# Expert output bias: from a small product in every expert block to one product of gates and bias rows behind the last block

## What is computed

```python
def moe(h, w_router, b_router, w1, b1, w2, b2):
    logits = (xf @ w_router) + b_router
    top_val, top_idx = lax.top_k(logits, TOP_K)        # 4 of 32
    gates = jax.nn.softmax(top_val, axis=-1)
    ...
    def expert_block(args):
        tok, e = args
        xb = xf[tok]
        act = clamped_swiglu(xb @ w1[e] + b1[e])
        return act @ w2[e] + b2[e]
    y = lax.map(expert_block, ...)
    y = y * buf_g[:, None]                             # each row times its gate
    out = jax.ops.segment_sum(y, buf_tok, num_segments=T)

h = h + moe(rmsnorm(h, ffn_norm), ...)
h = rmsnorm(h, final_norm)
```

## Time and profile before

| what | value |
|---|---|
| median of three runs | 1431.04 us |
| profiled execution, its own time | 1431.11 us |
| its span, first to last instruction | 1429.3 us |
| PE busy | 1302.9 us, 91% |
| DVE, ACT, POOL busy | 670.1, 291.4, 284.3 us |
| DMA, mean | 322 GB/s |
| granted clock of TensorE, mean | 0.963 |

### The profile page before, as it was taken

One profiled execution on the slowest core, in us unless ns is written; L12 is line 12 of the kernel. 1 busy time (PEld: TensorE's weight loads), 2 busy tenths in 40 slices (PEclk: granted clock), 3 DMA queues, 4 the chain that ended last, 5 costly groups with the idle time before them and its releaser, 6 DMA issues.

```text
span 1429.3 us, 36690 instructions
## 1 busy us (share of the span) xinstructions
PE 1302.9 (91%) x13312; PEld 623.7 (44%) x13313; DVE 670.1 (47%) x2257; ACT 291.4 (20%) x578; POOL 284.3 (20%) x455
## 2 busy tenths in 40 slices
PE   4999999989288997899999999997999899999992
PEld 2655666555233442344444444442444344444441
DVE  3015333664644553355555555553455355555555
ACT  3102223432011111111111111111111111111113
POOL 5400000000012222122222222222222122222221
PEclk9999999999589999999999999998999999999996
DMA  9520001617478999999999998999999999999995
GB/s 317 157 50 1 1 1 63 236 27 312 158 313 337 415 417 418 419 416 416 417 418 417 417 417 319 378 413 417 419 416 417 422 416 417 417 418 417 415 416 185
DMA packets 59808, 459.65 MB, mean 322 GB/s; under 512 B 8420, under 2 KB 8804, under 8 KB 27012
## 3 DMA queue, kind: packets, MB, share of 16 engines
q1 hardware_dynamic: 51220, 436.63, 73.8%
q0 software_dynamic: 8176, 22.36, 6.0%
q10 hardware_dynamic: 384, 0.26, 0.1%
HBM read 440.72 MB, written 18.51 MB: 321 GB/s over the span
## 4 chain that ended last, share of the span: by engine, by line
PE 83%; DMA 9%; DVE 4%; issue 2%; ACT 1%; POOL 0%; SPq 0%; DVEq 0%; POOLq 0%; ACTq 0%
PE PS L1546 37%; PE PS L1573 19%; DMA sb_arena<-in_w 7%; PE PS L1227 4%; PE PS L1233 4%; PE PS L1583 2%; PE PS L1230 2%; PE PS L1231 2%; PE PS L1422 2%; PE PS L1447 1%; PE PS L1521 1%; PE PS L1589 1%; PE PS L1553 1%; PE PS L1329 1%; PE PS L1395 1%
## 5 line engine op out<-in xcount | busy, mean ns | idle before, releaser
L1546 PE MATMUL PS<-sb_arena,sb_work 128*32 128x512 f32 x5184 | 586.7, 603 | 35.3 <-DMA sb_arena<-in_w 28.6
L1546 PEld LDWEIGHTS PS<-sb_arena,sb_work 128*32 128x32 f32 x5184 | 174.2, 111 | 398.1 <-issue 347.4
L1573 PE MATMUL PS<-sb_arena,sb_work 128*32 128x256 f32 x5184 | 296.5, 380 | 4.6
L1129 DVE TENSOR_SCALAR sb_work<-PS 128x256 f32<-128x256 f32 x81 | 34.4, 425 | 395.8 <-PE PS L1553 395.8
L1573 PEld LDWEIGHTS PS<-sb_arena,sb_work 128*32 128x32 f32 x5184 | 166.3, 110 | 111.1 <-issue 19.4
L769 ACT ACTIVATE sb_work<-PS 128x256 f32<-128x256 f32 x81 | 31.1, 384 | 810.9 <-PE PS L1583 810.9
L1142 DVE TENSOR_SCALAR sb_work<-PS,sb_gates 32x256 f32<-32x256 f32 x324 | 155.2, 479 | 15.0 <-PE PS L1573 0.8
L534 POOL TENSOR_TENSOR sb_sm<-sb_sm 128x1 f32<-128x1 f32 x85 | 16.9, 199 | 676.9 <-DVE sb_gidx L1120 676.9
L1097 DVE TENSOR_SCALAR sb_slots<-sb_ca,sb_b,sb_rk 128x128 bf16<-128x128 f32 x344 | 96.5, 370 | 59.0 <-issue 58.2
L543 POOL DMA_INDIRECT accd<-sb_work,sb_sidc x81 | 111.1, 1371 | 12.5 <-issue 1.1
L767 ACT ACT_TABLE_LOAD x81 | 103.9, 1283 | 1.4
(11 more groups left out here) (246 smaller groups left out, 1165.8 us busy)
## 6 DMA issues: line engine op xcount, KB each, us to landing
sb_arena<-in_w SPq DMA_DIRECT2D x192, 2048.0 KB
sb_arena<-in_w_in SPq DMA_DIRECT2D x6, 2048.0 KB, 21.4
sb_arena<-in_x SPq DMA_DIRECT2D x8, 512.0 KB, 9.6
sb_arena<-in_w_out SPq DMA_DIRECT2D x2, 2048.0 KB, 13.1
accd<-sb_arena SPq DMA_DIRECT2D x4, 512.0 KB, 7.6
xfd<-sb_arena SPq DMA_DIRECT2D x4, 512.0 KB, 5.8
sb_arena<-accd SPq DMA_DIRECT2D x4, 512.0 KB, 5.0
out<-sb_arena SPq DMA_DIRECT2D x4, 512.0 KB, 3.5
```

The costliest lines, as they stand in the source:

```text
L1546: last = mm(PS[group(c), b, :].rearrange("p (a n) -> p a n", a=2), xT[:, k % 2, group(k // 2)], w[:, k, :, c, :], start=k == 0, stop=False)
L1573: last = mm(PS[group(n), 4, 0:QD], actT[:, k % 2, group(k // 2)], w[:, k, n * QD:(n + 1) * QD], start=False, stop=k == KT - 1)
```

## The change

The bias `b2` no longer enters the blocks. `ball` keeps the two parts of `b1`; POOL splits two thirds of the rows that it split before. The gates of a tile are now kept in `gk` ([128 tokens, 32 experts] for each of four tiles). Between the routing and the first block PE turns them (four transposes into PSUM bank 0) and ACT copies the result to `gT` ([32, 512]). In a block the four products at L1589 are gone, and the first product of `down` starts the sum.

Behind the last block SP loads `b2` as it is ([32, 1024], 128 KB) ahead of the final gain. PE multiplies: for each token tile and each half of the columns `gT` times `b2` (eight products, 32 rows deep, 512 columns wide, one PSUM bank each), then for each of the same eight banks the identity times the loaded rows of `accd` (128 rows deep), which adds those rows to the bias in PSUM. ACT squares from PSUM and no longer from SBUF, and DVE's product with the gain reads PSUM and waits until ACT has read the tile (`fin_sq`), since both read the same banks.

```diff
@@ SP
+            sp.wait_ge(gT_done, 1)
             w1_load(1, 1)
...
             sp.wait_ge(up_done, nb)
+            sp.dma_start(fb2, I["b2"]).then_inc(b2_in, 16)
             sp.dma_start(fgain, I["final_norm"].to_broadcast([P, D])).then_inc(acc_in, 16)
@@ POOL
-            for c in range(3):
-                src = I["b1"][:, c * D:(c + 1) * D] if c < 2 else I["b2"]
-                pool.dma_start(bchunk, src).then_inc(bch_in, 16)
+            for c in range(2):
+                pool.dma_start(bchunk, I["b1"][:, c * D:(c + 1) * D]).then_inc(bch_in, 16)
@@ ACT
+            act.wait_ge(gT_done, 1)
+            act.activation(gT[:, :], PS[0:NE, 0, :], ACT.Copy).then_inc(gT_ready, 1)
             xT_copy(0, 0)
...
             act.preload_act_table_set("natural_log_exp_and_others")
+            act.activation(sm[:, 20:21], ones1, ACT.Copy).then_inc(copies_over, 1)
             for u in (0, 2):
                 for t in (u, u + 1):
-                    act.wait_ge(x_in[t], 48)
-                    act.activation(fsq[:, t, :], fh[:, t, :], ACT.Square, accum_out=ss[:, t:t + 1]).then_inc(fin_sq, 1)
+                    act.wait_ge(sum_done, t + 1)
+                    act.activation(fsq[:, t, :].rearrange("p (b n) -> p b n", b=2), PS[:, 2 * t:2 * t + 2, :],
+                                   ACT.Square, accum_out=ss[:, t:t + 1]).then_inc(fin_sq, 1)
@@ DVE
-                step(nc.vector.tensor_reduce(gd, ohg.rearrange("p k e -> p e k"), AX.X, ALU.add))
+                nc.vector.tensor_reduce(gk[:, t, :], ohg.rearrange("p k e -> p e k"), AX.X, ALU.add)\
+                    .then_inc(gk_ready, 1)
+                dve.wait_ge(gk_ready, t + 1)
...
+            nc.vector.memset(nx, 0.0).then_inc(rows_over, 1)
             dve.wait_ge(acc_in, 16)
-            for u in (0, 2):
-                for t in (u, u + 1):
-                    dve.wait_ge(x_in[t], 48)
-                    nc.vector.tensor_tensor(fg[:, t, :], fh[:, t, :], fgain, ALU.mult).then_inc(fin_gain, 1)
+            for t in range(TT):
+                dve.wait_ge(fin_sq, t + 1)
+                nc.vector.tensor_tensor(fg[:, t, :].rearrange("p (b n) -> p b n", b=2), PS[:, 2 * t:2 * t + 2, :],
+                                        fgain.rearrange("p (b n) -> p b n", b=2), ALU.mult).then_inc(fin_gain, 1)
@@ PE, down and finish_block
-                                  w[:, k, n * QD:(n + 1) * QD], start=False, stop=k == KT - 1)
+                                  w[:, k, n * QD:(n + 1) * QD], start=k == 0, stop=k == KT - 1)
...
                 pe.wait_ge(sel_ready, g + 2)
-                for n in range(Q):
-                    mm(PS[group(n), 4, 0:QD], selb[:, b, :], ball[:, 2 * D + n * QD:2 * D + (n + 1) * QD],
-                       start=True, stop=False)
                 pe.wait_ge(actT_ready, g + 1)
@@ PE, ahead of the blocks
+            pe.wait_ge(gk_ready, TT)
+            for t in range(TT):
+                last = nc.tensor.transpose(PS[0:NE, 0, t * P:(t + 1) * P], gk[:, t, :], ident)
+            last.then_inc(gT_done, 1)
             turn_x(0, 0, 0)
             slot_product(1)
+            pe.wait_ge(gT_ready, 1)
@@ PE, behind the blocks
+            pe.wait_ge(b2_in, 16)
+            for t in range(TT):
+                if t == 2:
+                    pe.wait_ge(rows_over, 1)
+                    pe.wait_ge(copies_over, 1)
+                for n in range(2):
+                    mm(PS[:, 2 * t + n, :], gT[:, t * P:(t + 1) * P], fb2[:, n * 512:(n + 1) * 512],
+                       start=True, stop=False, skip_group_check=True)
+            for t in range(TT):
+                pe.wait_ge(x_in[t], 48)
+                for n in range(2):
+                    last = mm(PS[:, 2 * t + n, :], ident, fh[:, t, n * 512:(n + 1) * 512],
+                              start=False, stop=True, skip_group_check=True)
+                last.then_inc(sum_done, 1)
```

More of the change, by code:

```diff
@@ L189, in build @@
         fg = arena[:, 9 * D:13 * D].rearrange("p (t d) -> p t d", t=TT)
+        fb2 = arena[0:NE, 13 * D:14 * D]
         wo = slot(2)
@@ L229, in build @@
         rt = left[:, 656:664]
+        gk = arena[:, o - HF * NKEY:o - HF * NKEY + P].rearrange("p (t e) -> p t e", t=TT)
         work = sb("work", [P, 5 * 512])
@@ L279, in build @@
         ident = ca[:, C_ID:C_ID + P]
-        ball = sb("ball", [P, 3 * D], BF16)
+        ball = sb("ball", [P, 2 * D], BF16)
+        gT = sb("gT", [NE, T])
         g6 = sb("g6", [P, TT, NE, 6], BF16)
@@ L341, in build @@
         added = sem("added")
+        gk_ready, gT_done, gT_ready = sem("gk_ready"), sem("gT_done"), sem("gT_ready")
+        b2_in, rows_over, copies_over, sum_done = sem("b2_in"), sem("rows_over"), sem("copies_over"), sem("sum_done")
         w1_full = [[sem(f"w1_full{par}{c}") for c in range(4)] for par in range(2)]
@@ L1020, in _ @@
                 step(nc.vector.tensor_tensor(ohg, e4.unsqueeze(2).to_broadcast([P, TOPK, NE]), oh, ALU.mult))
-                step(nc.vector.tensor_reduce(gd, ohg.rearrange("p k e -> p e k"), AX.X, ALU.add))
-                step(nc.vector.tensor_copy(g6[:, t, :, 0], gd))
-                step(nc.vector.tensor_tensor(gd, gd, g6[:, t, :, 0], ALU.subtract))
+                nc.vector.tensor_reduce(gk[:, t, :], ohg.rearrange("p k e -> p e k"), AX.X, ALU.add)\
+                    .then_inc(gk_ready, 1)
+                dve.wait_ge(gk_ready, t + 1)
+                step(nc.vector.tensor_copy(g6[:, t, :, 0], gk[:, t, :]))
+                step(nc.vector.tensor_tensor(gd, gk[:, t, :], g6[:, t, :, 0], ALU.subtract))
                 step(nc.vector.tensor_copy(g6[:, t, :, 1], gd))
```

## The result

The changed kernel takes 1456.11 us (median of 4 runs, 1455.39 to 1460.86) beside 1431.39 us for the kernel before on the same chip (4 runs, 1430.64 to 1434.6): a ratio of 1.0177, with a 95% interval of 1.0158 to 1.0197. The forecast was 1441.8 us, its range 1437.0 to 1447.5. The direction was right; 14 us were missing.

What follows compares the result with a forecast made beforehand. PE was taken to set the time in 52 blocks, the DMA engines from 930 to 1132 and up to 579 us. Terms 0 + 0 + 10.8 on a median of 1431.04 gave 1441.8 us, range 1437.0 to 1447.5.

Steps and rivals of the forecast that it cites:

- A loss is excluded, since nothing is added to a block: Expert blocks, four products removed: no loss possible, at most 0.09 or 0.18 us gained a block.
- Edit 1: Four products less in each of 81 blocks: 0 us.
- they fill a wait that stays when they go: Before `down` in a block: the four products only fill the wait for ACT's copy, so removing them gives 0.
- Its own sign: In a block of the profile after: `down` still starts 0.17 to 0.18 us behind the end of ACT's copy.
- 52 blocks that PE sets: Two stretches, 582 to about 920 us (29 blocks) and 1135 to 1401 us (23), where PE alone sets the time.
- The DMA engines set it from 930 to 1132: Expert blocks from 930 to 1132 us: the DMA engines, not PE, set the time.
- Edit 2: Work ahead of the blocks (four transposes, ACT's copy, waits): hidden in PE's 5.0 us idle gap, 0 us.
- Edit 3: The end, PE's 32 float32 passes, then square and gain product: the end moves by +10.8 us.
- the 2.1 us for the clock's rise: PE's passes at the end: 2.1 us added to 14.0 because the clock starts at half after idle time.
- The rival for it: At the end, products only 32 rows deep leave the clock at half: 6.9 us more, 1448.7; chance 0.09.
- new code on PE: PE's new instructions behind the loop aren't at hand: up to 5.5 us more, 1447.3; chance 0.10.
- the stall at 437 us: PE's 5.48 us issue stall falls otherwise with another code length: up to 5.5 us back, 1436.3 to 1441; chance 0.07.

Runs made afterwards that it cites:

- the wait for w2 first: The changed kernel with the wait for w2 and its register work ahead of the wait for ACT's copy: 1449.08 us, ratio 1.0127.
- every wait on a row of its own: The kernel before with the wait for w2's first half and its register work moved to the second of the four products: 1425.34 us, ratio 0.9954.

## Why the prediction was wrong

- **"A loss is excluded, since nothing is added to a block"** is the step that failed in Edit 1, and it put 0 to 0.18 us of gain where there was 0.11 of loss. The count of products was right, and so was "they fill a wait that stays when they go"; but I listed instructions and not the waits that they carry. One of the products carried a wait, the order of instructions with its waits showed where it would go, and I had read that order without them. The runs show it both ways: the wait without the loss of products (+8.6 us by the ratio), the products back without the loss (6.8 us less than the changed kernel by medians that were not taken side by side, 7.3 by the ratios). Its own sign (`down` 0.17 to 0.18 us behind the end of ACT's copy) came out as 0.29.
- **Where a block counts.** I took 52 blocks that PE sets, which would make 5.7 us at 0.109 each. The loss came in every one: from the block at 581.98 (580.95 with the change) to the last at 1400.31 (1406.71) there are 68 blocks, 818.33 and 825.76 us, 7.4 more, 0.109 each. "The DMA engines set it from 930 to 1132" was thus wrong for a loss: the waits for weights stayed as long as they were (28.6 and 27.2 us in all), only later. That each load waits for a buffer that PE's block frees would explain it; no run took that apart. A gain came through in part: between the same two blocks the trace with 11.74 us a block takes 0.5 us more than that of the kernel before instead of 2.7 less (581.69 to 1400.48), and those with 11.65 take 4.8 (with products, 584.93 to 1398.46) and 7.1 less (without, 581.79 to 1393.04) where 68 blocks would give 8.8.
- **Edit 2, 0**: 1.0 us off. The first `up` took 8.42 us instead of 9.05, the granted clock from 394 to 400 was 0.58 instead of 0.50, and the first block's copy came at 414.71 instead of 415.77. The new transposes stand shortly before; whether they did it wasn't tried, and the time at 581 varies by more between runs (584.93 in one).
- **Edit 3, +10.8**: the count of passes, the chain of square and gain product, the arrival of the rows and the start 7.3 us behind the last `down` all held. The step that failed is the 2.1 us for the clock's rise, which measured 8.9 (22.9 us for the 32 passes instead of 16.1): I took it from products 128 rows deep, and "the depth of 32 rows instead of 128 changes nothing in the count of columns" is true and beside the point. The rival for it was there, with the right price (6.9 forecast, 6.8 measured) and a chance of 0.09, on the argument "no row has them". No row is no evidence for either side, and a chance nearer one half would have been honest.
- **The sum.** Forecast 10.8; measured 24.2 of span: 6.2 loop (7.4 in the blocks, 1.0 off ahead of them, 0.2 off in the last), 6.8 clock, 10.7 as forecast, 0.5 behind the last product with the gain. None of the rivals with new code on PE or the stall at 437 us came: the stall is 5.33 us now, 5.48 before.

## What to carry to other kernels

An instruction that is removed leaves its waits behind. Before calling a removal free, list the waits of the rows around it, before and after, and look for rows with two: on a chain that every block runs through, one such row cost 0.11 us a block here, and spreading the waits over earlier instructions that aren't on the chain brought 0.46% with no work removed. Work that fills a wait is free where it stands; moved to an end where nothing covers it, it has to be paid in full. And where a stretch of PE follows idle time, ask what kind of products will raise the clock: price them from a row of the same shape, or carry both clocks in the forecast.

## What the runs showed of the hardware

- TensorE stayed at 1.2 GHz (0.50) through 14 us of float32 products 32 rows deep in which it was never idle, and rose some 4 us into the same products at 128 rows, zeros included (the window from 1425 has 0.86, the products begin at 1421.90). It fell from 1.00 to 0.50 under 32 row deep products, about 6 us behind the last deep one. The Trainium skill, TensorE: Matmul & The Clock Gate, Part 1, ties the clock to how busy the engine has been lately; by these runs busy time alone doesn't settle it, since the same columns behind the same idle time (7.32 and 7.30 us) came out differently with 32 and with 128 rows in use.
- The instruction for the second wait lasts 51 ns, and cost 0.11 us a block where it stood between a release and register work, and 0.09 where it stood between the release and the weight load of `down` (11.74 with the wait for w2 first, 11.65 with every wait on a row of its own).
- The register work between a wait and `down` was on the chain too: with it and every second wait out of the way `down` starts 0.06 us behind the end of ACT's copy (1241.65 to 1241.71), where it took 0.18 before and 0.29 in the changed kernel.
